# Two attentions of a transformer layer pair: the queries' two-part split moves from GpSimd to ScalarE and VectorE

## What is computed

```python
def chunked_relpos_attention(q, k, v, rel_bias):      # "banded": a chunk of 64 queries sees 576 keys
    ...
    def one_chunk(c):
        ...
        s = jnp.einsum('bqhd,bkhd->bhqk', qc, kc).astype(jnp.float32) * scale + bias[None]
        s = jnp.where(valid[None, None], s, NEG)
        p = jax.nn.softmax(s, axis=-1).astype(v.dtype)
        return jnp.einsum('bhqk,bkhd->bqhd', p, vc)

def dsa_sparse_attention(q, k, v, iq, ik, iw):        # "sparse": one key head, 256 selected keys per query
    ...
        s = jnp.einsum('bqhd,bqkd->bqhk', qb, ks).astype(jnp.float32) * scale
        s = jnp.where(sel_valid[:, :, None, :], s, NEG)
        p = jax.nn.softmax(s, axis=-1).astype(v.dtype)
        return jnp.einsum('bqhk,bqkd->bqhd', p, vs)
```

## Time and profile before

| what | value |
|---|---|
| time, median of 3 runs | 4643.75 us (4641.72 to 4645.11) |
| the profiled execution's own time | 4644.84 us |
| span of its trace, first to last instruction | 4643.1 us |
| banded attention in the trace | about 3389 to 3695 us |
| sparse attention in the trace | about 3701 to 4160 us |
| TensorE busy over the span | 4297.9 us (93%) |
| VectorE, ScalarE, GpSimd busy over the span | 2483.1, 1398.7, 771.9 us |
| mean granted TensorE clock | 0.958 |

### The profile page before, as it was taken

One profiled execution on the slowest core, in us unless ns is written; L12 is line 12 of the kernel. 1 busy time (PEld: TensorE's weight loads), 2 busy tenths in 40 slices (PEclk: granted clock), 3 DMA queues, 4 the chain that ended last, 5 costly groups with the idle time before them and its releaser, 6 DMA issues. The chain is left out here.

```text
span 4643.1 us, 62582 instructions
## 1 busy us (share of the span) xinstructions
PE 4297.9 (93%) x22581; PEld 2626.7 (57%) x22581; DVE 2483.1 (53%) x5846; ACT 1398.7 (30%) x2865; POOL 771.9 (17%) x774
## 2 busy tenths in 40 slices
PE   7799999999986999979799999999978899989998
PEld 5465656565642333335365454545447778767775
DVE  4543443434344333336478999999956565432222
ACT  1133333333320111113267210010256667650000
POOL 0001010010103555532132000000021111000001
PEclk9799999999987999989899999999989999999999
DMA  9755555656415877746564444444552332133221
GB/s 290 233 177 164 177 164 166 175 158 180 148 55 219 307 257 268 267 137 213 153 170 125 149 116 136 129 116 111 165 150 78 73 91 59 51 111 94 90 90 63
DMA packets 686981, 705.07 MB, mean 152 GB/s; under 512 B 196440, under 2 KB 539696, under 8 KB 673776
## 3 DMA queue, kind: packets, MB, share of 16 engines
q1 hardware_dynamic: 595152, 495.68, 36.0%
q0 software_dynamic: 63696, 185.05, 11.6%
q10 hardware_dynamic: 27856, 20.71, 1.4%
HBM read 770.36 MB, written 135.36 MB: 195 GB/s over the span
## 5 line engine op out<-in xcount | busy, mean ns | idle before, releaser
L1972 PE MATMUL l_unit<-l_xT,l_w 128*128 128x512 f32 x2048 | 909.5, 593 | 32.8 <-DMA l_xT<-mid_xn3T 29.3
L1972 PEld LDWEIGHTS l_unit<-l_xT,l_w 128*128 128x128 f32 x2048 | 387.3, 190 | 469.5 <-issue 457.1
L2073 DVE TENSOR_SCALAR_CACHE_REDUCE l_work<-l_score,l_trial 128x384 bf16<-128x384 f32 (+1 forms) x434 | 617.2, 1475 | 8.9
L419 PE MATMUL f_ring<-f_win,f_hT 128*128 128x512 f32 x1024 | 466.9, 613 | 15.5 <-issue 8.8
L1338 PE MATMUL e_ph<-e_gateup,e_rowsT 128*64 128x512 f32 x1536 | 343.6, 600 | 7.0 <-DVE e_rowsT L1505 5.0
L419 PEld LDWEIGHTS f_ring<-f_win,f_hT 128*128 128x128 f32 x1024 | 196.0, 195 | 257.7 <-issue 244.9
L2414 DVE CUSTOM_DVE_ANT_0 sparse_scores<-sparse_s,sparse_pen 128x512 f32<-128x512 f32 (+3 forms) x320 | 182.6, 608 | 183.1 <-PE sparse_s L126 167.2
L2530 PE MATMUL o_branch<-o_y,w_branches 128*128 128x128 f32 x2048 | 232.9, 276 | 14.1 <-DMA o_gates<-mid_gzT 14.1
L2530 PEld LDWEIGHTS o_branch<-o_y,w_branches 128*128 128x128 f32 x2048 | 232.7, 193 | 21.0 <-issue 21.0
L2542 PE MATMUL o_out<-w_last,o_merged 128*128 128x512 f32 x512 | 225.2, 598 | 5.2 <-POOL o_merged L2512 5.2
L527 PE MATMUL f_ring<-f_wout,f_trio 128*128 128x512 f32 x512 | 225.7, 599 | 1.4 <-DVE f_trio L900 1.4
(11 more groups left out here) (389 smaller groups left out, 6914.0 us busy)
## 6 DMA issues: line engine op xcount, KB each, us to landing
f_win<-in_w_in SPq DMA_DIRECT2D x64, 2048.0 KB, 8.3
l_w<-in_w_in SPq DMA_DIRECT2D x144, 512.0 KB, 4.1
f_win<-in_w_in SPq DMA_DIRECT2D x128, 256.0 KB, 5.0
f_wout<-in_w_ada SPq DMA_DIRECT2D x24, 1024.0 KB, 12.2
mid_ys<-e_out SPq DMA_DIRECT2D x48, 512.0 KB, 5.4
f_win<-in_w_in SPq DMA_DIRECT2D x16, 1024.0 KB, 6.9
mid_gzT<-l_out SPq DMA_DIRECT2D x64, 256.0 KB, 4.1
o_gates<-mid_gzT SPq DMA_DIRECT2D x16, 1024.0 KB, 7.8
```

Of the source, the lines that this page charges most:

```text
L419: mm = nc.tensor.matmul(to[:, :], hT[:, k, :], w[:, k, :], start=(k == 0), stop=(k == KD - 1))
L1972: mm = nc.tensor.matmul(pu[n % 2][:, :], w[:, n % WB, k, :], xT[:, t % 2, k, :], start=(k == 0), stop=(k == KD - 1))
L2073: V.tensor_scalar(unread, score(b), at_least(b), None, op, ALU.add, accum_out=count[:, b:b + 1])
```

## The change

GpSimd's program is taken out of both attentions. ScalarE now rounds a block's queries (`q_head`, a Copy activation of 128x1024) and VectorE computes the rest (`q_rest`). The first block's split stands ahead of the first key pieces on both engines. The split of block i+1 stands in iteration (i, 1): on ScalarE behind `probs` of heads 4 and 5 and the key piece of that step if there is one, on VectorE behind `rowmax` of heads 4 and 5 and that key piece. A new semaphore, `q_heads_ready`, lets VectorE wait for ScalarE. The waits that GpSimd had (queries landed, matmuls of two blocks before done) stand in front of ScalarE's instruction.

```diff
-            @block.gpsimd
-            def _(pool):
-                for i in range(NB):
-                    u = i % 2
...
-                    head(nc.gpsimd, q_parts[0][:, u, :, :], q[:, u, :, :])
-                    pool.drain()
-                    rest(nc.gpsimd, q_parts[1][:, u, :, :], q[:, u, :, :], q_parts[0][:, u, :, :]).then_inc(q_ready, 1)
...
@@ scalar
+                def split_q(i):
+                    u = i % 2
+                    if banded and i == 0:
+                        act.wait_ge(g.band_q_loaded, 32)
+                    else:
+                        act.wait_ge(q_loaded[u], 32 * (i // 2 + (0 if banded and u == 0 else 1)))
+                    if i >= 2:
+                        act.wait_ge(qk, first[i - 1])
+                    settle(g, act)
+                    nc.scalar.activation(q_parts[0][:, u, :, :].bitcast(F32R), q[:, u, :, :], ACT.Copy).then_inc(q_head, 1)
...
+                split_q(0)
                 for h in range(KH):
                     split_k(0, h)
...
                     for grp, h in k_prep(i)[p - 1:p] if p else ():
                         split_k(grp, h)
+                    if p == 1 and i + 1 < NB:
+                        split_q(i + 1)
...
@@ vector
+                def split_q(i):
+                    v.wait_ge(q_head, i + 1)
+                    rest(V, q_parts[1][:, i % 2, :, :], q[:, i % 2, :, :], q_parts[0][:, i % 2, :, :]).then_inc(q_ready, 1)
...
+                split_q(0)
                 if banded:
                     v.wait_ge(g.band_bias_ready, 16 * PAIRS)
                 ready(0)
...
                     for grp, h in k_prep(i)[p - 1:p] if p else ():
                         split_k(grp, h)
+                    if p == 1 and i + 1 < NB:
+                        split_q(i + 1)
```

More of the change, by code:

```diff
@@ L2173, in stage_attend @@
             sem, "consts_loaded qk_done scores_read max_ready probs_ready probsT_done probsT_read pv_done inverse_ready inverse_rows inverse_rows_read gated".split())
-        q_ready, k_head, k_ready, raw_free = map(sem, "q_parts_ready k_heads_ready k_parts_ready raw_free".split())
+        q_head, q_ready, k_head, k_ready, raw_free = map(sem, "q_heads_ready q_parts_ready k_heads_ready k_parts_ready raw_free".split())
         q_loaded, pen_loaded, gate_loaded, stored = ([sem(f"{n}_{u}") for u in range(2)] for n in ("q_loaded", "pen_loaded", "gate_loaded", "stored"))
@@ L2244, in _ @@
                     sp.dma_start(g.w_last[:], g.w_out_2[0].rearrange("(k p) n -> p k n", p=P)).then_inc(g.w_out_loaded, 16)
-            @block.gpsimd
-            def _(pool):
-                for i in range(NB):
-                    u = i % 2
-                    if banded and i == 0:
-                        pool.wait_ge(g.band_q_loaded, 32)
-                    else:
-                        pool.wait_ge(q_loaded[u], 32 * (i // 2 + (0 if banded and u == 0 else 1)))
-                    if i >= 2:
-                        pool.wait_ge(qk, first[i - 1])
-                    settle(g, pool)
-                    head(nc.gpsimd, q_parts[0][:, u, :, :], q[:, u, :, :])
-                    pool.drain()
-                    rest(nc.gpsimd, q_parts[1][:, u, :, :], q[:, u, :, :], q_parts[0][:, u, :, :]).then_inc(q_ready, 1)
             @block.tensor
```

## The result

The changed kernel takes 4676.74 us (median of 4 runs, 4673.6 to 4679.3) against 4642.74 us (4 runs, 4636.26 to 4645.11): a ratio of 1.0075, 95% interval 1.0058 to 1.0093. The forecast was 4681, slower. The profiled execution took 4674.49 us with a span of 4672.7; the spans differ by 29.6 us, and it is these 29.6 that the two traces can explain.

The account below looks back on a forecast made before the run. The prediction took TensorE to bound the kernel, with VectorE and ScalarE in a loop with it. 4644.8 + 41.3 (shifts) + 6 (clock) - 11 (contention) = 4681 us, range of 8 in 10 4656 to 4712.

Parts of the forecast that it names:

- What bounds the kernel: Three banded blocks without a split key piece: TensorE busy 48.0 of 48.5 us, so no idle time to win back.
- Rival 3: In all blocks the loop takes up half of each shift: 4651 us, within 0.2%; chance 0.09.
- The two durations: New instructions: ScalarE's head of 1024 columns takes 1.05 us, VectorE's rest 1.22, worked out from other column counts.
- The shifts: VectorE's later read of head 6's scores delays blocks: 21.3 us banded and 20.0 sparse, +41.3 us.
- Without a key piece: Six banded blocks (3, 7, 11 to 14) without a key piece at pair 1: 1.6 us late each, 9.6 us.
- The 1.2 that the sum has for one chunk: Sparse blocks 0 to 3: head 6's maximum comes 1.75 us late, costing 1.2 us each, 4.8 together.
- Contention: VectorE instructions stretched beside GpSimd's, in both attentions, return to normal length: -11 us, bounded by 0 and -14.
- The clock: Banded blocks with key pieces from block 4 on: 3.5 more half-clock stretches at 1.7 us each, +6 us (0 to 10).
- The lower bound of 4664: Whole kernel: the forecast's own lower bound, 4664 us, given as 22 of the 30 shifts at 0.5 us less.
- Rival 1: Clock also falls in the other blocks, nine stretches of 1.7 us, and all six banded ones double: 4700 us; chance 0.17.
- Rival 2: Both attentions: VectorE's rest hides under its waits for scores, only the freed VectorE counts: 4634 us; chance 0.06.
- At the stage starts: Start of the two attention stages: 1.1 us of gain from ending VectorE's stretching by GpSimd, within the -11 us.

Follow-up runs that it names:

- e1: Changed kernel with only the queries of blocks 0 and 1 split, later blocks using old buffer contents; 4638.5 us, 0.9984 of the kernel before.
- e12: The kernel before, word for word, run again for a second trace; 4644.1 us in one run.
- e11: The kernel of e1, word for word, run again for a second trace; 4636.1 us in one run.
- e4: Changed kernel with ScalarE's query head one step earlier and VectorE's rest ahead of the key piece; 4633.8 us, 0.9973 of the kernel before.
- e3: Changed kernel with ScalarE rounding only blocks 0 and 1's queries, VectorE making every rest without waiting for ScalarE; 4656.1 us, 1.0021 of the kernel before.
- e7: e4 with ScalarE's key head one step later and VectorE's key rest one step behind that; 4600.9 us, 0.9917 of the kernel before.

## Why the prediction was right

- **What bounds the kernel.** Right, and it carried the rest: three blocks had 0.5 us of idle time in 48.5, and the late reads in them appeared nearly in full. Rival 3, the loop taking up half, fell in banded blocks 12 and 13 (1.5 us late of 1.6 forecast).
- **The two durations.** 1.04 and 1.225 us for 1.05 and 1.22. Interpolating by columns held, though the rows had other partitions.
- **The shifts.** Without a key piece 8.9 for 9.6 us; sparse, two chunks, 1.73 each for 1.8; three chunks 0.8 to 1.7 for 1.6; four chunks 0.8, 0.6 and 0.4 for 0.8 each. The forecast's small excess is in the handing on: ScalarE's head starts some 0.1 us before the row of the exponentials ends (3645.53 against 3645.66), and for wide blocks the exponentials' place moves, which one row for three blocks couldn't tell. In banded block 3 there was 0.7 only. Its heads have one chunk of 512 columns, since the second chunk comes from block 4 on, so the sum should have priced it as a sparse block of one chunk. Sparse block 3, which has the same shape, shows the same: in both, steps 2 and 3 are longer by 0.35 to 0.4 us each. The 1.2 that the sum has for one chunk is too much for this shape as well.
- **Contention.** Right in kind and about right in size: all stretched rests and copies are gone, and e1 gives 8.1 us with the first blocks' splits still in, for a forecast of 11. A part of that is clock. Where e12 and the first trace differ by a stretched rest alone, in banded blocks 4 and 8, it is worth 1.5 and 1.6 us.
- **The clock: the term that was mis-sized.** The sum had +6 us, for 3.5 more stretches at 1.7 each. Measured, the time at half clock in banded blocks 4 to 10 is 23.9 us in both traces: two stretches became double (blocks 5 and 6), and block 9, which had two, has none. And a single stretch costs 0.46 us rather than 1.7, as e11 and e12 show, since the halved clock fell on steps in which TensorE waits anyway. A second one right behind it is dearer, near the 1.7 (e4's block 9, e3's blocks 9 and 10); it is the count that was wrong there. In banded blocks 0 to 3, for which the sum had nothing, 4.5 us more are at half clock (30.2 for 25.7). Without the +6 the blocks' sum is +31, and the traces show +30.4. That the two are so close is in part luck: the banded blocks with a key piece grew by 6.1 us where the sum has 3 without the clock, and all the others together by 4 less than it has for them. The lower bound of 4664 is also not what its text says: 22 shifts at 0.5 less give 4670, and the rest is the +6 taken out as well.
- **Rival 1**, the clock falling after idle times of 1.5 us: it fell behind none of them (1.24 to 1.26 in banded blocks 7 and 11 to 14, 1.44 to 1.86 in sparse blocks 3 and 5 to 8).
- **Rival 2**, faster. Its condition was named rightly: 2.3 us have to fit ahead of the first read of head 6. The changed kernel doesn't meet it; e4 does, by the place alone, and gets the 4634 that the rival gave. The rule of the Trainium skill (page "SBUF — State Buffer", section "Who interferes with whom") on VectorE and GpSimd is borne out: with no GpSimd instruction beside it the key rest takes 0.69 us in every one of 32 cases, and in e12, where the key rest came first, it was GpSimd's instruction that grew. What the prediction quotes of the rule covers instructions with two SBUF inputs; the two stretched copies have one, and they are at 0.43 us again too. The advice of the Trainium skill (page "Perfetto Trace Analysis", section "Optimizing GPSIMD Operations") to prefer other engines holds in e4 and e7, and fails in the changed kernel, where it costs 34 us: it says nothing of the place in the other engines' queues.
- **At the stage starts** I had put 1.1 us of gain. In the sparse stage 0.4 us of it came: from the rounding of the key piece to the first scores it takes 1.55 us instead of 1.96. In the banded stage there is none, for a reason that the prediction left out. The first scores do start earlier, at 3392.42 instead of 3392.96. But ScalarE rounds eight key pieces in a row at the start, 4.26 us, and only behind them comes the one load of its tables in these stages; the query head of 1.06 us now stands ahead of all of it. The load, before and after:

```profile
3393.29 1.28 ACT L2362 ACT_TABLE_LOAD   x1
```

```profile
3394.43 1.28 ACT L2358 ACT_TABLE_LOAD   x1
```

The load ends 1.1 us later, the first exponentials wait for it, and the first evacuation is at 3396.78 against 3396.77.

## What to carry to other kernels

When work moves to an engine whose queue others wait for, its total time says little; follow the one chain through its new place: when its input is ready, what stands behind it in the queue, and who waits for that. Two halves on two engines can each fit into idle time and still cost almost their whole length if the second waits for the first in the same step; put the producer a step ahead of the consumer. Then look for the same pattern in the code next to it, which here gave more than twice as much again (e7 is 39 us below the kernel before, e4 11, each against its own executions of it).

## What the runs showed of the hardware

**How long TensorE is idle doesn't alone say whether its clock falls.** In the earlier trace rows the clock was at 0.50 after 2.18 us of idle time. In banded block 9 after the change TensorE was idle for 3.30 us (row above), and the windows of that idle time and of the stretch behind it are

```profile
3585.70:3589.10 3.40, 0.10 (x2) 0.07 (x1) 2.64 (x5) 2.38 (x4) 0.00 (x0) 1.00 0.97 218
3589.10:3592.50 3.40, 3.40 (x37) 2.98 (x37) 1.56 (x9) 2.79 (x8) 0.00 (x0) 1.00 0.02 5
```

with PEclk 1.00 in both. It is so at shorter idle times too: in sparse block 8 the changed kernel kept 1.00 behind 1.86 us, and e3 fell to 0.50 behind 1.90. e1 and e11 have idle times of 2.2 to 2.8 us in their blocks with key pieces and one stretch at half clock in blocks 4 to 10; the kernel before has idle times of 2.2 to 2.8 us there too, and six or seven stretches. Their number repeated in a second execution of each kernel, their places did not. What decides it was not found.

**A single stretch at half clock is cheap where TensorE waits anyway** (0.46 us for 3.4, in two blocks), and two in a row are not: 6.8 us of it made e4's block 9 longer than e1's by 2.0.

**Of VectorE and GpSimd, the one that starts second is stretched.** Key rests that started 0.1 us behind a GpSimd rest of 2.37 took 2.8 us, those that started 0.1 us ahead of one took 0.69.
